# One step later: where the cross-attention pieces stand between the weight units on five queues

## The reference

```python
q = (h @ w_q).reshape(Bn, S, X_HEADS, X_HEAD_DIM)
k, v = jnp.split(m @ w_kv, 2, axis=-1)
s = jnp.einsum('bshd,bmhd->bhsm', q, k).astype(jnp.float32) * (X_HEAD_DIM ** -0.5)
p = jax.nn.softmax(s, axis=-1).astype(v.dtype)
o = jnp.einsum('bhsm,bmhd->bshd', p, v).reshape(Bn, S, D_MODEL)
return o @ w_o
```

## Time and profile before

| | |
|---|---|
| median of 3 runs | 848.38 us (847.22 to 849.62) |
| profiled execution | 849.62 us, span from first to last instruction 848.4 us |
| PE busy | 807.3 us, 95% of the span |
| DVE busy | 560.9 us, 66% |
| ACT busy | 416.1 us, 49% |
| mean granted clock of PE | 0.974 |

### The profile page before, as it was taken

The page is one execution under the profiler, slowest core; times in us unless marked ns, Lnnn a source line. Parts: engine busy times, 40 slices in busy tenths (PEclk is TensorE's granted clock), DMA queues, the critical chain, the costliest instruction groups (busy, mean ns, idle before and its releaser), DMA issues.

```text
span 848.4 us, 13025 instructions
## 1 busy us (share of the span) xinstructions
PE 807.3 (95%) x5300; PEld 734.4 (87%) x5300; DVE 560.9 (66%) x761; ACT 416.1 (49%) x610; POOL 83.3 (10%) x129
## 2 busy tenths in 40 slices
PE   2989999999997999999999999899999999999995
PEld 2889998989877999999989998688987999999994
DVE  4875887849964655656566798847555755555563
ACT  4444356644346463534447467547544644434441
POOL 6200960001200010000001000011000100000000
PEclk8998999989999999999999999999999999999998
DMA  9969777767563655555656654445534466565641
GB/s 308 363 211 303 267 252 262 245 237 274 175 197 107 191 185 184 180 182 188 195 179 180 180 164 151 136 144 171 192 103 147 124 199 198 179 194 183 190 150 49
DMA packets 83323, 163.70 MB, mean 193 GB/s; under 512 B 5424, under 2 KB 13808, under 8 KB 83264
## 3 DMA queue, kind: packets, MB, share of 16 engines
q1 hardware_dynamic: 81344, 157.31, 57.6%
q10 hardware_dynamic: 1424, 4.81, 1.6%
q0 software_dynamic: 496, 0.76, 0.3%
HBM read 161.81 MB, written 1.05 MB: 192 GB/s over the span
## 4 chain that ended last, share of the span: by engine, by line
PE 85%; ACT 6%; DVE 5%; issue 2%; POOL 1%; DMA 1%; SPq 0%; ACTq 0%; DVEq 0%; POOLq 0%
PE bank L1628 26%; PE bank L1629 25%; PE bank L1630 25%; ACT hi_ring L461 2%; DVE lo_ring L864 1%; PE bank L1789 1%; DVE ada_acc L896 1%; PE bank L1694 1%; PE bank L2094 1%; PE bank L2115 1%; PE bank L1667 1%; DVE x_residual L970 1%; DMA ada_ring<-in_w_ada 1%; ACT gates L516 1%; PE bank L1803 1%
## 5 line engine op out<-in xcount | busy, mean ns | idle before, releaser
L864 DVE TENSOR_TENSOR lo_ring<-raw_ring,hi_ring 128x1024 fp32r<-128x1024 f32 x248 | 304.7, 1233 | 196.0 <-ACT hi_ring L461 195.4
L461 ACT CAST hi_ring<-raw_ring 128x1024 fp32r<-128x1024 f32 x248 | 258.9, 1049 | 312.0 <-PE bank L1630 295.4
L1628 PE MATMUL bank<-h_hi,hi_ring 128*128 128x256 f32 x1008 | 292.6, 290 | 2.7 <-DVE h_lo L929 2.1
L1629 PE MATMUL bank<-h_lo,hi_ring 128*128 128x256 f32 x1008 | 289.4, 287 | 0.0
L1630 PE MATMUL bank<-h_hi,lo_ring 128*128 128x256 f32 x1008 | 289.1, 287 | 0.0
L1628 PEld LDWEIGHTS bank<-h_hi,hi_ring 128*128 128x128 f32 x1008 | 197.7, 196 | 5.7 <-issue 4.0
L1629 PEld LDWEIGHTS bank<-h_lo,hi_ring 128*128 128x128 f32 x1008 | 197.9, 196 | 0.8 <-issue 0.2
L1630 PEld LDWEIGHTS bank<-h_hi,lo_ring 128*128 128x128 f32 x1008 | 197.7, 196 | 0.0
L1628 PE MATMUL bank<-hi_ring,branch_hi 128*128 128x512 f32 x320 | 125.8, 393 | 0.1
L1629 PE MATMUL bank<-lo_ring,branch_hi 128*128 128x512 f32 x320 | 124.7, 390 | 0.0
L1630 PE MATMUL bank<-hi_ring,branch_lo 128*128 128x512 f32 x320 | 124.6, 389 | 0.0
(11 more groups left out here) (261 smaller groups left out, 952.3 us busy)
## 6 DMA issues: line engine op xcount, KB each, us to landing
raw_ring<-in_w_ff SPq DMA_DIRECT2D x128, 512.0 KB, 3.7
raw_ring<-in_w_in SPq DMA_DIRECT2D x64, 512.0 KB, 4.2
raw_ring<-in_w_out SPq DMA_DIRECT2D x16, 512.0 KB, 3.6
raw_ring<-in_w_xkv SPq DMA_DIRECT2D x16, 512.0 KB, 3.7
mem_v<-in_w_ada SPq DMA_DIRECT2D x12, 512.0 KB, 5.7
ada_ring<-in_w_ada SPq DMA_DIRECT2D x10, 512.0 KB, 4.7
mem_k<-in_w_ada SPq DMA_DIRECT2D x10, 512.0 KB, 5.5
raw_ring<-in_w_branch SPq DMA_DIRECT2D x8, 512.0 KB, 5.0
```

What stands on the lines that cost most here:

```text
L461: act.copy(m.hi[:, m.slot(u)], m.raw[:, m.slot(u)]).then_inc(s.hi_done, 1)
L864: dve.tensor_tensor(m.lo[:, m.slot(u)], m.raw[:, m.slot(u)], as_f32(m.hi[:, m.slot(u)]), ALU.subtract).then_inc(s.lo_done, 1)
L1628: pe.matmul(out, a_hi, b_hi, start=start, stop=False, skip_group_check=True)
L1629: pe.matmul(out, a_hi, b_lo, start=False, stop=False, skip_group_check=True)
```

## The change

The table of steps is shifted. On PE turn 0 moves from step 2 to 3, attend 1 from step 4 to 5, turn 2 from 5 to 6, attend 2 and turn 3 from 6 to 7, attend 3 from 7 to 8. ACT and DVE get matching steps, and there `cross_follow` now stands behind `after(...)` of the same step in place of ahead of it. Nothing is added or removed, on POOL and SP nothing moves. As three hunks on the three queues (the rest of the diff is of the same kind):

```diff
@@ act_program
-        if step == 2:
+        if step == 3:
             cross_turned(0)
         if step == 4:
             cross_exponentials(2)
-            cross_out(1)
             cross_exponentials(3)
         if step == 5:
+            cross_out(1)
+        if step == 6:
             cross_turned(2)
-        if step == 6:
+        if step == 7:
             cross_out(2)
             cross_turned(3)
-        if step == 7:
+        if step == 8:
             cross_out(3)
...
+            after(XQ + RING * c + j)
             if c == 1:
                 cross_follow(j)
-            after(XQ + RING * c + j)
...
-        cross_follow(RING + i)
         if i < len(XO_ORDER) - 1:
             after(XO + i)
+        cross_follow(RING + i)
@@ dve_program
-        if step == 1:
+        if step == 2:
             cross_normalize(0)
-        if step == 2:
             cross_normalize(1)
-        if step == 4:
+        if step == 5:
+            cross_out(1)
             cross_normalize(2)
-            cross_out(1)
             cross_normalize(3)
-        if step in (6, 7):
-            cross_out(step - 4)
+        if step == 7:
+            cross_out(2)
+        if step == 8:
+            cross_out(3)
@@ pe_program
-        if step == 2:
+        if step == 3:
             cross_turn(0)
-        if step == 4:
+        if step == 5:
             cross_attend(1)
-        if step == 5:
+        if step == 6:
             cross_turn(2)
-        if step == 6:
+        if step == 7:
             cross_attend(2)
             cross_turn(3)
-        if step == 7:
+        if step == 8:
             cross_attend(3)
```

## The result

The changed kernel takes 856.01 us (median of 10 runs, 853.73 to 861.93), the kernel before on the same chip 849.10 us (10 runs, 847.22 to 851.69). The ratio is 1.0088, 95% interval 1.0066 to 1.0109, that is 5.6 to 9.3 us slower. The forecast was 856.2, in a range of 853.2 to 859.2.

The account below looks back on a forecast made before the run. PE was taken as the bound, busy 66.00 of 66.00 us in the stage and waiting for nobody. Waits of 6.2 us plus one clock fall of 1.6 make 7.8, on the median 848.38: 856.2 us, range 853.2 to 859.2.

Parts of the forecast that it names:

- First wait, turn 0: PE waits 2.0 us at turn 0 for head 0's normalisation, late behind cast, table load, exponentials and subtraction.
- Second wait, attend 0: Directly behind turn 0, PE waits about 0.95 us for ACT to copy out the turned head.
- Third wait, XO+2: Attend 1 directly ahead of XO+2 has no covering unit; PE waits 2.1 us, or 1.7 with DVE free.
- Fourth, XO+4: Attend 2 and turn 3 ahead of XO+4: chain 3.24 us less their 2.08 us, a wait of 1.15 us.
- Sum of the waits: Four PE waits in the cross-attention stage, 2.0 + 0.95 + 2.1 + 1.15 = 6.2 us, bounds 4.5 and 7.0.
- The clock: Idle PE time brings one fall of the granted clock to half rate in the stage, costing 1.6 us.
- site 1: Turn 0 and attend 0: 2.95 us of idle around 0.35 us of work, the likeliest place for a clock fall.
- rival 1: Waits in the stage as computed but no fall of the clock: 854.6 us; chance 0.35.
- 259 us: Idle PE at 259 to 260 us precedes clock 0.50 at 262; site 1 was judged more like this than 548 us.
- The range: Whole time from 853.2 (waits 4.5, no fall) to 859.2 us (7.0 and two falls less run-to-run spread).
- The excursion that fell away: Turn 0 adjoins attend 0, sparing one excursion from the weight passes; worth 0.1 us at most, nothing subtracted.
- sparse stretches: Claim that falls of the granted clock follow stretches where PE has little work; a sparse enough one brings the fall.

Follow-up runs that it names:

- exp_early: Changed kernel with the exponentials of heads 0 and 1 ahead of the cast again, on ACT at step 1 only; stage 55.25 us against 56.57.
- table_early: Changed kernel with a small unused exponential at step 0 on ACT, so the table load falls into idle time; stage 55.31 us against 56.57.
- merged: Kernel before with attend 1 moved directly behind scores 3 on PE, ACT and DVE; stage 50.02 us against 50.03.

## Why the prediction was right, and where it wasn't

- **Bound by PE, nobody awaited.** Right. The one number from which all followed is the 66.00 of 66.00 us in the earlier trace rows; the same stretch has 60.47 now, and the part behind gave nothing back.
- **First wait, turn 0**: 2.0 forecast, 2.06 measured in the bracket; from start to start, as the next ones are counted, it is 2.15 (617.07 - 602.76 = 14.31, against 12.16 without the wait). The chain (slot wait, cast, table load, exponentials, cast, subtraction, normalisation) stands in the rows of ACT and DVE above with the lengths that were forecast, and `exp_early` and `table_early` moved two of its links.
- **Second wait, attend 0**: 0.95 forecast. Turn 0 to attend 0 takes 618.46 - 617.07 = 1.39, of which turn 0 is 0.35: 1.04. The bracket in the timeline (0.77) is shorter than what is lost, since a matmul's modelled end (618.46 - 0.77 = 617.69) lies behind the point up to which it costs PE (617.07 + 0.35 = 617.42).
- **Third wait, XO+2**: 2.1 forecast; attend 1 starts at 629.63, XO+2 at 633.25, so 3.62 against 1.54 undisturbed: 2.08. **Fourth, XO+4**: 1.15 forecast; 642.62 - 639.33 = 3.29 against 2.08: 1.21.
- **Sum of the waits**: 6.2 forecast, 6.54 measured, with 2.0 + 0.95 growing to 3.2 as the largest part of the gap (the hand-over to PE at turn 0, 0.14 us, for which I had put nothing, and a little at the one to attend 0).
- **The clock: the step that failed.** "I take one fall as likeliest, at site 1: +1.6 us" is not what the three profiles show; rival 1 (waits, no fall) is. The likeness that I drew with 259 us was read from one row. The idle time there is not longer at a stretch than that at site 1 (2.09 us against 2.06), but it is the last of three waits with only transposes between them, 4.32 us of idle in all:

```profile
256.38 1.10 PE L1667 MATMUL bank<-ident,gates 128*128 128x128 f32 x8 [1.86 <-DVE gates L915]
257.84 1.09 PE L1667 MATMUL bank<-ident,gates 128*128 128x128 f32 x8 [0.37 <-DVE gates L915]
261.03 0.36 PE L1628 MATMUL bank<-h_hi,hi_ring 128*128 128x256 f32 x1 [2.09 <-DVE h_lo L929]
```

  In size the term was wrong too: 2.4 to 3.0 us where a fall did come, since one fall was priced by the shorter kind of stretch.
- **Why the time came out all the same.** In part by luck: three misses cancel to 0.2 us. The median of the first three runs, from which I started, lies 0.7 us below that of the ten (848.38 against 849.10); the waits were 0.3 us too small; and of my 1.6 us for the clock the medians leave 856.01 - 849.10 - 6.54 = 0.4, which is 1.2 too much. By the ratio, 1.0088 or 7.5 us, 0.9 is left. A fall in a third of the executions would be worth 2.4 / 3 = 0.8 us on the average, but its existence isn't shown, and the interval (5.6 to 9.3 us) holds 6.5 and 7.8 alike: the time alone can't tell my forecast from rival 1.
- **The range.** Its upper bound is not the sum that it is said to be: 848.38 + 7.0 + 3.2 = 858.6, and the spread comes on top of that, not off it. The spread of single executions was set too small as well, 1.2 us to either side; 47 of the kernel before go from 846.75 to 851.69.
- **Edits at nothing.** Earlier casts brought nothing, as said. The excursion that fell away brought nothing either (`merged`: 0.01 us).

## What to carry to other kernels

Where one engine runs full and others feed it, a hand-written order is a set of covers: for each piece count what stands between it and its first reader, and compare that with the chain over the other queues. Here 3.24 us of chain costs nothing with a unit of 2.9 us and the piece's own 1.54 us in between, and without the unit it costs all that the 1.54 us doesn't cover, however idle the other engines look on the page. Put work that waits for a free slot behind work that is ready, not ahead of it, for a queue waits in order. And read a change of 1% by the length of its own stage in the profile, which repeated within 0.1 us here, rather than by the whole time, which scattered by 8. Here is one limit of that: a fall of the clock that comes in some executions only can't be seen in a profile of another.

## What the hardware showed that I had not expected

- A table load of 1.28 us moves with the order of the instructions: it is free where ACT is idle in front of it, and fully on the path behind a cast that waits (1.26 us back when placed early).
- The granted clock stayed at 1.00 over an idle time of 2.06 us followed by 0.35 us of transposes and another 0.77 us of idle, in three of three profiles, and fell to 0.50 in a wait of 3.01 us; half rate lasted from about 618 to 625 us, longer than the wait, and PE worked through most of it at half speed. The Trainium skill says that activity releases the throttle ("TensorE: Matmul & The Clock Gate", Part 1). The trace agrees in kind, with these two lengths.
- It also fell where PE shows no idle time at all. In the profile of before PE is busy 2.00 of 2.00 us from 96 to 98 us, with nine small matmuls (64 or 16 rows), and at 98 us the clock goes to half rate:

```profile
96.00:98.00 2.00, 2.00 (x9) 1.22 (x10) 0.49 (x2) 0.19 (x1) 1.76 (x4) 1.00 1.01 370
98.00:100.00 2.00, 2.00 (x11) 2.00 (x11) 1.97 (x7) 0.00 (x0) 1.84 (x3) 0.50 0.28 115
```

  So the "sparse stretches" of my prediction are not only those with idle time, and the busy share of a page does not tell where the clock will fall.
- Going from the float32r passes to float32 pieces and back once less in the stage saved nothing measurable (50.02 against 50.03 us).
